# Overflow blocks, output gathers and held-back weight slabs in a two-layer encoder with a grouped mixture of experts

## What is computed

```python
for l in range(2):
    x = x + g1 * mixer_l(modulate(rmsnorm(x), sh1, sc1))
    h = modulate(rmsnorm(x), sh2, sc2)
    x = x + g2 * grouped_moe(h, ...)          # router shared by the layers
return rmsnorm(x)

# grouped_moe: scores -> the best of 4 groups -> 2 experts of it per token
#   tokens sorted by expert, padded to blocks of 128 rows
#   y = (silu(xb @ w_gate[e]) * (xb @ w_up[e])) @ w_down[e]      for every block
#   out[token] += weight * y                                     two rows per token
```

## Time and profile before

| what | us |
|---|---|
| median of three runs | 1387.87 |
| the profiled execution's own time | 1388.95 |
| its span, first to last instruction | 1387.2 |
| TensorE busy (matmul) | 1278.2 (92%) |
| VectorE busy | 1033.7 (75%) |
| ScalarE busy | 680.4 (49%) |
| mean granted TensorE clock | 0.969 of full |

### The profile page before, as it was taken

One profiled execution on the slowest core, in us unless ns is written; L12 is line 12 of the kernel. 1 busy time (PEld: TensorE's weight loads), 2 busy tenths in 40 slices (PEclk: granted clock), 3 DMA queues, 4 the chain that ended last, 5 costly groups with the idle time before them and its releaser, 6 DMA issues.

```text
span 1387.2 us, 15640 instructions
## 1 busy us (share of the span) xinstructions
PE 1278.2 (92%) x5389; PEld 907.8 (65%) x5389; DVE 1033.7 (75%) x1415; ACT 680.4 (49%) x877; POOL 164.0 (12%) x169
## 2 busy tenths in 40 slices
PE   2999899989999999996899999999799999999876
PEld 2466765577777777753788854468777777777532
DVE  8679975477898888837766587856678898888253
ACT  3477402326667666614222167644366667666002
POOL 6000000010000000010000057710100000000200
PEclk9999999899999999999999999999899999999989
DMA  9727674257999999885465230022689999998651
GB/s 353 243 91 273 227 264 190 91 212 279 379 384 378 389 384 388 323 320 212 134 235 180 89 122 0 1 77 99 278 312 392 389 381 381 385 381 321 234 198 60
DMA packets 78116, 347.84 MB, mean 251 GB/s; under 512 B 12500, under 2 KB 12684, under 8 KB 69104
## 3 DMA queue, kind: packets, MB, share of 16 engines
q1 hardware_dynamic: 67184, 325.70, 62.7%
q0 software_dynamic: 7344, 16.68, 3.2%
q10 hardware_dynamic: 3536, 4.79, 0.9%
HBM read 334.15 MB, written 23.07 MB: 258 GB/s over the span
## 4 chain that ended last, share of the span: by engine, by line
PE 73%; DVE 13%; DMA 6%; ACT 4%; issue 3%; POOL 1%; SPq 0%; DVEq 0%; POOLq 0%; ACTq 0%
PE ps L1968 24%; PE ps L2101 8%; PE ps L1994 8%; PE ps L2001 6%; PE ps L1879 4%; DVE scratch L1054 3%; PE ps L1886 3%; PE ps L1954 2%; PE ps L1846 2%; DMA mod_ring<-y_rows,y_row 2%; PE ps L2145 2%; PE ps L2173 2%; PE ps L2159 2%; DMA x_res<-in_x_dram 1%; PE ps L1841 1%
## 5 line engine op out<-in xcount | busy, mean ns | idle before, releaser
L1968 PE MATMUL ps<-slab_ring_r,gate_rows_r 128*128 128x512 f32 x512 | 200.8, 392 | 0.0
L1476 DVE TENSOR_TENSOR slab_ring_r<-slab_ring,h_t_r 128x2048 fp32r<-128x2048 f32 x64 | 143.7, 2284 | 5.3 <-ACT h_t_r L858 5.3
L2101 PE MATMUL ps<-slab_ring_r 128*128 128x512 f32 x384 | 120.0, 394 | 6.3 <-DVE h_t_r L1111 6.3
L858 ACT ACTIVATE h_t_r<-slab_ring 128x2048 fp32r<-128x2048 f32 x64 | 118.7, 1903 | 0.0
L1994 PE MATMUL ps<-slab_ring,scratch 128*128 128x512 f32 x256 | 116.9, 600 | 1.5 <-ACT scratch L900 1.5
L1968 PEld LDWEIGHTS ps<-slab_ring_r,gate_rows_r 128*128 128x128 f32 x512 | 97.1, 190 | 18.5
L1968 PE MATMUL ps<-h_t_r,gate_rows_r 128*128 128x512 f32 x256 | 104.3, 407 | 4.9 <-DVE slab_ring_r L1476 4.9
L1968 PE MATMUL ps<-h_t_r,scratch_r 128*128 128x512 f32 x256 | 101.4, 396 | 0.0
L725 POOL TENSOR_SCALAR mod_ring<-mod_ring,row_rcp 128x512 f32<-128x512 f32 x48 | 76.9, 1614 | 204.7 <-DVE row_rcp L1732 204.6
L1476 DVE TENSOR_TENSOR slab_ring_r<-slab_ring,x_norm_r 128x2048 fp32r<-128x2048 f32 x32 | 73.1, 2287 | 19.3 <-ACT x_norm_r L858 19.3
L1476 DVE TENSOR_TENSOR slab_ring_r<-slab_ring,mod_ring_r 128x2048 fp32r<-128x2048 f32 x32 | 73.1, 2287 | 19.3 <-ACT mod_ring_r L858 19.3
(11 more groups left out here) (360 smaller groups left out, 2710.3 us busy)
## 6 DMA issues: line engine op xcount, KB each, us to landing
slab_ring<-in_expert_w_gate_dram SPq DMA_DIRECT2D x35, 2048.0 KB, 8.6
slab_ring<-in_expert_w_up_dram SPq DMA_DIRECT2D x35, 2048.0 KB, 10.1
slab_ring<-in_expert_w_down_dram SPq DMA_DIRECT2D x35, 2048.0 KB, 10.3
mod_ring<-in_mod_w_dram SPq DMA_DIRECT2D x40, 512.0 KB, 4.7
y_rows<-scratch SPq DMA_DIRECT2D x32, 512.0 KB, 10.5
slab_ring<-in_mod_w_dram SPq DMA_DIRECT2D x32, 512.0 KB, 4.8
slab_ring<-in_mod_w_dram SPq DMA_DIRECT2D x12, 1024.0 KB, 11.3
slab_ring<-in_w_qkv_dram SPq DMA_DIRECT2D x6, 2048.0 KB, 17.0
```

What stands on the lines that cost most here:

```text
L858: act.activation(top, w, ACT.Copy).then_inc(high_ready[c], 1)
L1476: tt_(rest, w, top.bitcast(F32), ALU.subtract).then_inc(low_ready[c], 1)
L1968: ins = pe.matmul(ps[:, bank, :], x, w, start=(kt == 0 and i == 0), stop=(kt == KT - 1 and i == 2))
L2101: ins = pe.matmul(ps[:, i % 6, :], x[:, kt, cut], y[:, k, :], start=(kt == 0 and n == 0), stop=(kt == KT - 1 and n == 2))
```

## The change

Four edits, in both layers' code unless said otherwise:

1. SP issues the first six slabs in the order (0,0), (0,1), (1,0), (0,2), (1,1), (1,2), and waits for the landing of the first row gather (`xs_filled[0]`) before the fifth of them in layer 0 and before the fourth in layer 1.
2. SP in layer 0 waits for all eight output gathers (`comb_filled[t]`, t = 0 to 3) after the last `y_rows` store and before the second and third `w_qkv` slab.
3. POOL gathers block 1's rows right after block 0's rows have been transposed, ahead of the wait for the stores and of the eight output gathers; this applies where `n_over` > 1.
4. VectorE: in layer 0 the order stays as it was, except that with two blocks or more block 1's `xst_over`, block 0's `over_y`, adds and block 1's mask would come before `combine(1..3)`. In layer 1 `over_hid(0)` comes before all combines; with two blocks or more the same steps of block 1 follow, then `combine(0..3)`, then `over_hid(1)`.

```diff
-            for e in range(2):
-                for c in range(3):
-                    sp.wait_ge(*free[3 * e + c])
-                    load_part(l, c, e, e)
+            order = ((0, 0), (0, 1), (1, 0), (0, 2), (1, 1), (1, 2))
+            for i, (e, c) in enumerate(order):
+                sp.wait_ge(*free[3 * e + c])
+                if i == 4 - l:
+                    sp.wait_ge(xs_filled[0], (NE // 2) * l * 16 + 16)
+                load_part(l, c, e, e)
...
                     if w == 1:
                         store(NE - 1, 1)
+                        for t in range(TT):
+                            sp.wait_ge(comb_filled[t], 32)
...
             gather_over(0)
+            with gp.If(n_over > 1):
+                gp.wait_ge(o["turned"], 1)
+                gather_over(1)
             for par in range(2):
                 gp.wait_ge(yb_stored[par], 16 * (NE // 2) * (l + 1))
...
-            with gp.Fori(0, MAX_OVER - 1) as k:
+            with gp.Fori(1, MAX_OVER - 1) as k:
...
+            def over_next(k):
+                xst_over(k)
+                over_y(k)
+                for t in range(TT):
+                    over_add(k, t)
+                over_mask(k)
...
-            combine(0)
+            if l == 0:
+                combine(0)
             with v.If(n_over > 0):
                 over_hid(0)
-            for t in range(1, TT):
+            with v.If(n_over > 1):
+                v.wait_ge(yb_stored[0], 16 * (NE // 2) * (l + 1))
+                over_next(1)
+            for t in range(1 - l, TT):
                 combine(t)
             v.wait_ge(yb_stored[0], 16 * (NE // 2) * (l + 1))
             with v.If(n_over > 1):
-                with v.Fori(1, MAX_OVER) as k:
+                over_hid(1)
+            with v.If(n_over > 2):
+                with v.Fori(2, MAX_OVER) as k:
                     with v.If(k < n_over):
-                        xst_over(k)
-                        over_y(k)
-                        for t in range(TT):
-                            over_add(k, t)
-                        over_mask(k)
+                        over_next(k)
                         over_hid(k)
```

## The result

The changed kernel takes 1371.38 us in the median of four runs (1369.0 to 1374.7); the kernel before took 1388.18 beside it. The ratio is 0.9876, 95% interval [0.986, 0.9891]: 16.8 us less. Forecast were 1365.2 us and a range from 1361.5 to 1373.0, so the sign and the range held, and the gain was 5.9 us smaller than its four terms.

What follows compares the result with a forecast made beforehand. TensorE is 73% of the last-ending chain; gains were sought where the chain leaves it, at both layers' expert-part starts and ends. 4.5 + 0.8 + 6.7 + 10.7 = 22.7 us, from 1387.87 to 1365.2, range 1361.5 to 1373.0.

Steps and rivals of the forecast that it cites:

- Layer 1's start: Start of layer 1's expert part (edit 1): store and first gather land sooner, second gather limits; 4.5 us gained, 3.1 to 5.8.
- 989.74 + 7.5 = 997.2: Layer 1's start: expert 1's row gather starts at 989.74 as before and takes the loop's median 7.5, landing at 997.2.
- a second row gather over 9 us: Sign named as showing the forecast wrong: the second row gather, at an expert part's start, taking over 9 us.
- Layer 0's start: Start of layer 0's expert part: expert 1's gather starts as before and lands at 310.3 against transposes at 311.15; 0.8 us.
- rival (a): Both layers' starts: held slabs slow the second gather to 11.5 us; gains 0.5 and -3.2, sum 14.7, 1373.2 us; chance 0.10.
- Rival (a2): Both starts gain nothing, the store's 11.52 having another cause (final gain's broadcast); sum 17.4, 1370.5 us; chance 0.02.
- Layer 0's end: End of layer 0's expert part (edit 2): output gathers land without `w_qkv` beside them, `over_y` starts 6.7 us earlier.
- tile 0 over 5 us: Sign named as showing the forecast wrong: output gathers for token tile 0, at layer 0's end, taking over 5 us.
- rival (c): After layer 0's end: `w_qkv` comes late behind SP's new wait and the kernel is slower than before; chance 0.03.
- Layer 1's end: End of layer 1's expert part (edits 3, 4): `over_hid(1)` at 1348.9 against 1359.65; 10.7 us, 9.1 with a slow mask product.
- Rival (b): Layer 1's end: output gathers land late, so VectorE's combines are the bound; 5 us come back, 1370 us; chance 0.04.
- Rival (d): Layer 1's end: the reorder doesn't act, or block 1's rows are still late, needing a gather over 30 us; chance 0.01.

Runs made afterwards that it cites:

- moving the hold: The changed kernel, but SP waits for the second row gather (expert 1's), before the fifth slab in both layers: 1366.42 us, ratio 0.9844; in another session 1363.5 us, 0.982.

## Why the prediction was right or wrong

**What bounds it: right.** The time came from three of the four places named, and nothing was lost elsewhere. Each of the four terms was too high, and the 16.8 us of the medians lie half a microsecond above the forecast's worst, 16.3. One term fell below its own bound; that the range held in spite of it is owed to the other three, and in that much to luck.

**Layer 1's start, 4.5 us: too high, 2.6 in the trace (2.2 with edit 1 alone), below the term's own bound of 3.1.** The first half of the step held: the store in 5.9 (said: under 6, though for two slabs in flight, where there was one), the first gather right at its list, TensorE idle for the second one only. The term that failed is "989.74 + 7.5 = 997.2", the second gather: I priced a gather beside freshly released slabs with the median of the loop's gathers, 7.5. It took 9.8. This one met three slabs that had been issued 3.5 us before it. It is the sign I had named as wrong ("a second row gather over 9 us"), and with it TensorE's idle was 4.27 and not 1 to 2.

**Layer 0's start, 0.8: nothing came.** At the transposes 0.1 us were lost, by expert 1's down product 0.2. The same term again, smaller: the gather took 7.74 and not 7.5 (0.2), and it went out 16.83 us behind the last store (302.92 - 286.09) instead of 16.33 (302.84 - 286.51), where I had it start unchanged (0.5). Another 0.2 is the row I compared with, which starts at 311.15 in the chain while the first of these matmuls starts at 310.99. It lies in the bounds given, -0.6 to 2.5.

**So rival (a) was half true.** It stood at 0.10 with landings of 11.5 and a sum of 14.7. The landings were 9.8 and 7.7, between the forecast's and the rival's, and moving the hold gave 3.7 and 2.9 us back at the two starts; by medians 5 to 8 us. The held slabs do take back part of the starts. "No gather of 28 took over 8.9" was true of gathers in a steady loop and no bound for one just behind a burst.

**Rival (a2) fell.** The cause it named, the broadcast behind the store, stayed where it was (1.2 us behind), and the store landed in 5.9. Layer 1's 512 KB stores took 2.6, 5.9, 9.1 and 11.5 us with none, one, two and four slabs still in flight, and one gather 3.3 or 9.8. The Trainium skill ("DMA: Bandwidth & Descriptors", section "Queues, rings and completion order") says that each DMA engine goes round the queues that hold work, one packet at a time; a store that shared its engines in equal turns would not pass twice its own transfer, about 4 us by my estimate from that page. The 5.9, 9.1 and 11.5 do not agree with equal shares. How packets are filled could explain a smaller share for the small transfer, but no run here shows the packets' order.

**Layer 0's end, 6.7: 5.9 in the trace, 6.3 with edit 2 alone.** The sign "tile 0 over 5 us" was just passed: its two gathers went out at 614.8 and 616.10, and the second landed after 5.3 us and not after the 3.5 to 4.5 of the forecast, so `combine(0)` ended at 624.06, 0.4 behind the up product, and `over_hid(0)` 0.6 behind. The cover on the other side was as thin as the step warned: the last combine ended 0.56 us ahead of the down product (632.93 against 633.49), and `over_y` came 0.38 behind that product. The step also took the down product at full clock; in three of the eight profiles with edit 2 it was not, and then 1.6 us more of the term are gone. `w_qkv` went out at 630.28 (said: about 631) and was not late, so rival (c) fell.

**Layer 1's end, 10.7: 9.7, and 9.45 alone.** The order of events is as forecast to within a microsecond. The mis-sized term is the mask product: I took 7.13 for it behind 2.7 idle, "nearer to" the row with 2.56, and it took 8.61 to 8.83 in each of the six profiles that had this idle. I had named 9.1 for this case. Rival (b) fell: the last combine ended 0.1 us behind the up product, not 2. Rival (d) fell too; the case without edit 3 shows what its "rows late" would have cost, 14.6 us, with a gather of 19.4 and not of 30.

**The sum.** 22.7 forecast; 18.0 in the trace, the difference being 1.9 and 1.0 at the starts (layer 1, layer 0), 0.8 and 1.0 at the ends (layer 0, layer 1). 16.8 in medians. The remaining 1.2 us between trace and medians is less than what one program's runs differ by, and I don't settle it.

## What to carry to other kernels

A small transfer that starts a stage should find no bulk transfer in flight; but when bulk loads are held back for it, hold them for the last small transfer on the path and not for the first, and check that the first use of the held load is far enough away (here, with the moved hold, 13.7 us behind the issue in layer 1 and 11.7 in layer 0). When steps of one engine are reordered so that a late input comes first, everything that used to cover its wait is queued behind it: move the input's producer forward first, which alone is worth nothing here, and then change the order. Price a transfer by rows from the same neighbourhood of traffic, not by the median of its kind in a steady loop.

## What the runs showed of the hardware

- The same eight matmuls of layer 0's last expert (0.75 idle before them) took 5.40 us in two profiles of twelve and 3.70 in the others, and layer 1's likewise in two others; sixteen took 8.83 or 7.13; eight transposes 1.97 or 1.16. The slow ones run at a granted clock of 0.50 from their start or within half a microsecond of it, and the long ones are back at 1.00 before they end. Behind 2.72 or 2.73 idle the mask product began at half clock in six profiles of six. Behind 2.56, and once behind 2.94 (layer 0 of the run with edit 3 alone), it ran at full clock; behind 2.04 it began at half clock once. Idle time alone did not decide it, and runs of one program differ by 3 to 10 us (1383.9 to 1394.4 for the kernel before in one session).
- Small matmuls ahead of the slow product brought it to full clock in both places tried, one profile each. On the path they cost more than that gave (3.83 us for thirty-two); under a wait they cost nothing (1.95 us for sixteen).
- A 512 KB row gather at an expert part's start took 3.3 to 4.4 us with no slab in flight, 7.5 to 9.9 beside slabs issued 2.8 to 3.8 us before it, and 19.4 behind eight gathers and beside slabs.
